# RWKV inverses kept with their halves exchanged, their increments issued in four array quadrants alternately

## The chip, the core and the metric

The kernel runs on one core of a Trainium2 chip. The metric is device time in microseconds (us) of one execution. The kernel before took 2090.66 us, the median of three runs (2089.09 to 2099.26). A change of 0.5% is 10.5 us.

A core has five engines with instruction queues of their own: TensorE (PE; its weight loads are shown as PEld), VectorE (DVE), ScalarE (ACT), GpSimd (POOL) and SyncE (SP, which issues transfers). They wait for each other through semaphores. TensorE writes to PSUM, eight banks of 512 fp32 columns on 128 partitions, and DVE and ACT read PSUM.

## What is computed

The program runs two blocks, one after the other. The first mixes a gated MLP branch and an RWKV-7 branch; the second has a latent attention (MLA) layer and a state-space (S5) layer. The change touches the RWKV-7 branch alone, whose core is a recurrence over 512 tokens for 8 heads of width 64:

```python
def step(S, inp):
    r_t, w_t, k_t, v_t, a_t, b_t = inp
    sa = jnp.einsum('bhij,bhj->bhi', S, a_t)
    S = S * w_t[:, :, None, :] + sa[..., None] * b_t[:, :, None, :] + v_t[..., None] * k_t[:, :, None, :]
    y = jnp.einsum('bhij,bhj->bhi', S, r_t)
    return S, y
```

## The kernel before

**Chunks and units.** The recurrence is cut into 8 chunks of 64 tokens. Inside a chunk it becomes products of 64x64 matrices and the inverse of a unit triangular one. Two heads make a unit (`q` or `i`, 0 to 3), and inside it `e` (0 or 1) is the head. For one head the 8 chunks lie as 4 pairs (`tt`), the even chunk of a pair on partitions 0 to 63, the odd one on 64 to 127, so a tile of 128 x 256 holds eight 64x64 matrices.

**A quadrant.** A 64x64 matmul uses a quarter of the 128x128 array: the 64 rows on which its operands lie, and the 64 columns that lead to the output's partitions. Here "0 to 1" means operands on partitions 0 to 63 and the output on 64 to 127.

**The inverse.** `products_pe` computes, for each chunk, the matrix A in both orientations and two products with r. `z0_dve` and `zt0_dve` mask the near diagonal of A, add the identity, and so start the inverse Z and its transpose ZT, kept in one tile `ZZ` (index 0 and 1). Then five levels double the block size of the inverse. At each level `u_pe` multiplies the masked A (`AL`, made by POOL) by Z, 8 matmuls for each head; ACT copies the result to `UA` (`u_act_`); `dz_pe` makes the increments of Z and ZT from `UA` and `ZZ`, 8 matmuls each for each head; and DVE adds both to `ZZ` in one operation of 512 columns (`dz_dve`, L1344). At level 5 only ZT is needed. At level 2 `u_pe` also multiplies `AKT` by v into the other half of the same bank, and one copy of 512 columns (L1283) takes both. `akt_pe` makes AKT into the place of the products once DVE has read them.

**Two quadrants, four quadrants.** All these level matmuls go through `turns` (L1193): even chunk 0 to 0, odd chunk 1 to 1, and so on alternately, so only two of the four quadrants are used. `product_pe` (L1177) goes over both heads and both chunk parities in turn: its operands lie on half `e` and its output on half `odd`, so it uses all four quadrants, and writes the two heads' results to two banks.

**Banks.** Before, X of head e (A, then the increments) is bank e and Y of head e (the transposed A, then U) is bank 2 + e.

**Order of work.** The order on every engine is written out by hand in `rwkv_pe`, `rwkv_act`, `rwkv_dve` (L1519, L1582, L1630). Between the steps of unit i stand the state recurrence of unit i - 1 (`state_pe`, `state_dve_`, one step for each chunk), the operands of unit i + 1 (`prep_...`), the normalisation of unit i - 2 (`gn_...`) and pieces of a vector times matrix product that the second block needs (`vec_rows_pe`, L337: 32 small matmuls of about 1 us, from weights that SP loads into a ring). Engines run their queues in order, so an instruction that waits holds all behind it.

Of the kernel before, what the change touches and what calls it, by code (L numbers as in the profile page):

```python
# [20 lines left out]
P = 128  # L21
# [162 lines left out]
def build(nc, io, known):  # L184
# [6 lines left out]
    with memory:  # L191
# [971 lines left out]
        def products_pe(pe, q):  # L1163
# [13 lines left out]
        def product_pe(b, a, lhs, rhs):  # L1177
            for c in range(NCHUNK):
                tt, odd = divmod(c, 2)
                cs = slice(c * CHUNK, (c + 1) * CHUNK)  # L1180
                for e in range(2):
                    ins = nc.tensor.matmul(psum[half(odd), b + e, a + tt * CHUNK:a + (tt + 1) * CHUNK], lhs[half(e), cs], rhs[half(e), cs],
# [3 lines left out]
        def akt_pe(pe, q):  # L1186
# [4 lines left out]
            pe_count.up("rw", q, "AKT")  # L1191

        def turns(b, a, lhs, rhs):  # L1193
            for tt in range(TT):
                for odd in range(2):
                    ins = nc.tensor.matmul(psum[half(odd), b, a + tt * CHUNK:a + (tt + 1) * CHUNK], lhs(half(odd), tt), rhs(half(odd), tt),  # L1196
                                           start=True, stop=True)
            return ins

        def u_pe(pe, q, level):  # L1200
            for e in range(2):
# [7 lines left out]
                if level == 2:  # L1209
                    pe.wait_ge(*at("rw", q, ("U_copied", 1), e))  # L1210
                    pe.wait_ge(*at("rw", q, "AKT_masked", e))
                    turns(2 + e, 256, lambda h, tt: AKT[h, tt, :], lambda h, tt: tms[q % 2][h, tt, 3, half(e)])
                pe.wait_ge(*at("rw", q, ("AL", level), e))
                turns(2 + e, 0, lambda h, tt: AL[h, level % 2, tt, :], lambda h, tt: ZZ[h, 0, tt, :]).then_inc(pe_done, 1)
                pe_count.up("rw", q, ("U", level), e)

        def dz_pe(pe, q, level):
            for e in range(2):
# [5 lines left out]
                if level < LEVELS:  # L1224
                    turns(e, 0, lambda h, tt: ZZ[h, 1, tt, :], lambda h, tt: UA[h, 0, tt, :])
                turns(e, 256, lambda h, tt: UA[h, 0, tt, :], lambda h, tt: ZZ[h, 1, tt, :]).then_inc(pe_done, 1)
                pe_count.up("rw", q, ("dZ", level), e)

        def w_pe_(pe, q):
            for e in range(2):  # L1230
# [3 lines left out]
                for tt in range(TT):  # L1234
                    for part in range(2):
                        for odd in range(2):
                            h = half(odd)
                            src = tms[q % 2][h, tt, 0, half(e)] if part == 0 else UA[h, 1, tt, :]
                            ins = nc.tensor.matmul(psum[h, 2 + e, tt * P + part * HEAD:tt * P + (part + 1) * HEAD], ZZ[h, 1, tt, :], src,
# [3133 lines left out]
```

## Time and profile before

| | |
|---|---|
| median of three runs | 2090.66 us |
| the profiled execution's own time | 2087.72 us |
| its span, first to last instruction | 2085.9 us |
| instructions in the span | 42823 |
| the four RWKV units | about 205 to 397 us of the span |
| TensorE busy over the span | 1970.8 us (94%) |
| VectorE busy over the span | 1509.0 us (72%) |

A row of the timeline gives the start in us from the span's start, the time to the end of the last of the merged instructions, the engine, the line of the kernel, the operation, output and inputs, their shapes and the count; in brackets stand the idle time ahead of it and who ended it. An fp32 matmul of the program shows as two passes, each a weight load (PEld) and a MATMUL (PE): 8 matmuls are x16. Their ends are modelled, so a rate is read from the distance between starts.

### The profile page before, as it was taken

The numbers are of one execution on the slowest core, as the hardware profiler recorded it, in microseconds if no ns is written. First come the engines' busy times: TensorE is split into PE (matmuls) and PEld (weight loads), VectorE is DVE, ScalarE is ACT, GpSimd is POOL, SyncE is SP. The second block draws the span as 40 slices with busy tenths as digits, with TensorE's granted clock in tenths as the row PEclk, the third lists the DMA queues.
The fourth block names the chain that finished last, engine by engine and source line by source line (L and its number), as shares of the span: only waits on it lengthen the run. The fifth ranks groups of instructions, "written<-read, shape, count | busy, mean of one in ns | idle before, by whom it ended". The sixth has DMA issues, their size and how long they took to land.

```text
span 2085.9 us, 42823 instructions
## 1 busy us (share of the span) xinstructions
PE 1970.8 (94%) x17574; PEld 1609.5 (77%) x17574; DVE 1509.0 (72%) x2103; ACT 912.9 (44%) x1540; POOL 516.6 (25%) x419
## 2 busy tenths in 40 slices
PE   7999898899999999999999979999989999999997
PEld 6787777777885656655579958888767799999885
DVE  3366665468994677688869866888884789898844
ACT  3325543344324444444465365555443544343423
POOL 2553221140005999300001121111111111111000
PEclk9999999999999999999999989999999999999998
DMA  9222344332452222112138858999964433333321
GB/s 366 86 92 71 124 144 144 145 133 74 157 191 92 71 91 86 61 64 79 66 136 327 294 217 236 311 305 303 323 206 167 142 102 102 103 104 114 137 91 41
DMA packets 127507, 317.89 MB, mean 152 GB/s; under 512 B 12129, under 2 KB 59105, under 8 KB 120913
## 3 DMA queue, kind: packets, MB, share of 16 engines
q1 hardware_dynamic: 114048, 248.65, 35.7%
q0 software_dynamic: 10672, 53.14, 7.0%
q10 hardware_dynamic: 2592, 13.37, 1.6%
q8 instruction: 140, 2.29, 0.4%
q14 instruction: 55, 0.44, 0.1%
HBM read 238.69 MB, written 76.41 MB: 151 GB/s over the span
## 4 chain that ended last, share of the span: by engine, by line
PE 78%; DVE 10%; issue 4%; ACT 4%; DMA 3%; POOL 1%; SPq 1%; ACTq 0%; POOLq 0%; DVEq 0%
PE psum L524 15%; PE psum L3785 14%; PE psum L2017 7%; PE psum L3209 5%; PE psum L2983 5%; PE psum L2640 5%; PE psum L2603 3%; PE psum L1196 3%; PE psum L2615 2%; PE psum L3379 2%; PE psum L337 2%; PE psum L3438 1%; PE psum L3329 1%; PE psum L2691 1%; PE psum L3185 1%
## 5 line engine op out<-in xcount | busy, mean ns | idle before, releaser
L3209 PE MATMUL psum<-h,u_w 128*128 128x256 f32 (+1 forms) x768 | 157.5, 349 | 7.3 <-DVE h L3137 5.2
L524 PE MATMUL psum<-h_split,in_w 128*128 128x512 f32 x600 | 139.1, 391 | 1.5 <-POOL in_w L513 1.5
L3209 PEld LDWEIGHTS psum<-h,u_w 128*128 128x128 f32 x768 | 118.0, 190 | 27.1 <-issue 10.9
L3742 POOL TENSOR_TENSOR ring<-ring 128x1024 f32<-128x1024 f32 x16 | 54.1, 3383 | 319.1 <-DVE xT L3736 319.1
L524 PEld LDWEIGHTS psum<-h_split,in_w 128*128 128x128 f32 x600 | 111.8, 188 | 27.3 <-ACT prev L860 2.1
L513 POOL TENSOR_TENSOR u_w<-ring,u_w 128x512 fp32r<-128x512 f32 x42 | 53.9, 1283 | 276.2 <-ACT u_w L501 240.9
L506 DVE TENSOR_TENSOR w_split<-ring,w_split 128x512 fp32r<-128x512 f32 x54 | 40.4, 748 | 86.3 <-ACT w_split L501 85.9
L2017 PE MATMUL psum<-x_high,ring_split 128*128 128x512 f32 x272 | 101.1, 393 | 0.0
L2640 PE MATMUL psum<-area,ckv_tm 128*128 128x512 f32 (+1 forms) x256 | 100.4, 545 | 0.0
L2738 DVE TENSOR_REDUCE early<-psum 128x1 f32<-128x768 f32 (+1 forms) x96 | 74.8, 780 | 32.2 <-PE psum L2615 29.6
L513 POOL TENSOR_TENSOR in_w<-ring,in_w 128x512 fp32r<-128x512 f32 x50 | 77.4, 1548 | 79.2 <-ACT in_w L501 77.0
L524 PE MATMUL psum<-split,w_split 128*128 128x512 f32 x384 | 89.7, 397 | 4.5 <-DVE w_split L506 4.5
L3785 PE MATMUL psum<-split,w_split 128*128 128x256 f32 x688 | 89.5, 283 | 1.3 <-ACT w_split L3756 1.3
L524 PEld LDWEIGHTS psum<-split,w_split 128*128 128x128 f32 x384 | 73.7, 192 | 20.2 <-DVE w_split L506 4.7
L2772 ACT ACTIVATE area<-psum 128x768 f32<-128x768 f32 x64 | 51.9, 811 | 84.6 <-PE psum L2629 83.6
L2640 PEld LDWEIGHTS psum<-area,ckv_tm 128*128 128x128 f32 x256 | 47.4, 190 | 51.3 <-issue 48.9
L3785 PEld LDWEIGHTS psum<-split,w_split 128*128 128x128 f32 x688 | 85.4, 191 | 1.7 <-ACT w_split L3756 1.7
L3785 PE MATMUL psum<-split,x_high 128*128 128x256 f32 x592 | 77.5, 284 | 2.4 <-DVE x_high L3764 2.4
L501 ACT ACTIVATE w_split<-ring 128x512 fp32r<-128x512 f32 x54 | 34.1, 631 | 103.2 <-PE psum L524 100.6
L2017 PE MATMUL psum<-ctx_high,ring_split 128*128 128x256 f32 x272 | 78.3, 288 | 0.0
L3785 PEld LDWEIGHTS psum<-split,x_high 128*128 128x128 f32 x592 | 72.8, 188 | 4.0 <-DVE x_high L3764 2.9
L2017 PE MATMUL psum<-h_low,ring_split 128*128 128x256 f32 (+1 forms) x272 | 70.1, 340 | 0.0
(530 smaller groups left out, 5247.0 us busy)
## 6 DMA issues: line engine op xcount, KB each, us to landing
ring<-in_s_glu SPq DMA_DIRECT2D x64, 512.0 KB, 3.3
ring<-in_w_mod SPq DMA_DIRECT2D x48, 512.0 KB, 5.4
c_pow<-made_c_pow SPq DMA_DIRECT2D x32, 576.0 KB, 5.1
ring<-in_s_in SPq DMA_DIRECT2D x32, 512.0 KB, 6.7
b_pow<-made_b_pow SPq DMA_DIRECT2D x15, 1024.0 KB, 10.5
ring<-in_w_in SPq DMA_DIRECT2D x25, 512.0 KB, 3.3
table<-made_table SPq DMA_DIRECT2D x32, 384.0 KB, 6.6
made_c_pow<-area POOLq DMA_DIRECT2D x10, 1152.0 KB, 5.7
```

Source lines behind the costliest of these rows:

```text
L513: nc.gpsimd.tensor_tensor(rounded(buffer(u, 1)), source(u), buffer(u, 0), ALU.subtract).then_inc(pool_done, 1)
L524: ins = nc.tensor.matmul(out, rounded(buffer(u, w)[:, ks]), values(x, k), start=(first and k == 0 and n == 0), stop=(last and k == UNIT_K ...
L1196: ins = nc.tensor.matmul(psum[half(odd), b, a + tt * CHUNK:a + (tt + 1) * CHUNK], lhs(half(odd), tt), rhs(half(odd), tt), start=True, stop ...
L2017: ins = nc.tensor.matmul(o, weights, h2_part(x, k, a, n), start=(k == 0 and w == 0 and x == 0), stop=(k == KD - 1 and w == 1))
L2603: mm(o, q_abs_of(h, u, q_part), rounded(ckv_parts[c_part][:, a:a + m]), start=(q_part == 0 and c_part == 0), stop=False)
L2640: ins = mm(o, ckv_tm[:, k, :], pt[:, k, :], start=(k == 0), stop=(k == kt - 1))
L2738: v.tensor_reduce(sm[:, n % 3, 0:1], scores_of(n), AX.X, ALU.max).then_inc(dve_done, 1)
L2772: nc.scalar.activation(dst, psum[:, 6:8, 0:3 * P].rearrange("p b (k c) -> p b k c", k=3), ACT.Copy).then_inc(act_done, 1)
L2983: ins = nc.tensor.matmul(mla_out_part(m, a, a + HALF), weights, rounded(values), start=(k == 0 and w == 0 and x == 0), stop=(k == KE - 1 a ...
L3209: ins = nc.tensor.matmul(o, rounded(u_w[:, u % 4, w, kk * P:(kk + 1) * P]), h3_part(x, k)[:, a:a + size], start=(k == 0 and n == 0), stop= ...
L3742: nc.gpsimd.tensor_tensor(left_plain(i, "S3"), left_plain(i, "A11"), left_plain(i, "S3"), ALU.subtract).then_inc(pool_done, 1)
L3785: ins = nc.tensor.matmul(product_of(i, q), left[:, k * P:(k + 1) * P], rounded(rounded_chunks[:, low_n if x else high_n, k, :]), start=(w ...
```

## The change

The transposed A that feeds `AL`, the A that starts Z, and with them `Z` and `AL`, are kept with the chunks of a pair exchanged: the even chunk on partitions 64 to 127. The U product then goes 0 to 1 and 1 to 0 and comes out in the natural places, the increment of Z goes 0 to 1 and 1 to 0 again, and the increment of ZT 0 to 0 and 1 to 1 as before. In `dz_pe` the two increments are now issued alternately, two matmuls of the one and two of the other, into two banks (X of head e is now bank 2e, Y is 2e + 1). ZT stays natural, so it needs a transposed A in the natural places: a fifth product of 16 matmuls (`at_natural_pe`) is computed into X ahead of AKT, and DVE masks it from PSUM instead of from the copy in `AT`. At level 2 the AKT product goes to the bank of X, so ACT copies it apart from U.

```diff
         def X(e, a=0, n=TT * CHUNK):
-            return bank(e, a, a + n)
+            return bank(2 * e, a, a + n)
         def Y(e, a=0, n=TT * CHUNK):
-            return bank(2 + e, a, a + n)
+            return bank(2 * e + 1, a, a + n)
...
             for b, lhs, rhs in ((0, a_cm, b_cm), (2, b_cm, a_cm)):
-                product_pe(b, 0, lhs, rhs).then_inc(pe_done, 1)
+                product_pe(b, 0, lhs, rhs, crossed=True).then_inc(pe_done, 1)
...
+        def at_natural_pe(pe, q):
             for e in range(2):
                 pe.wait_ge(*at("rw", q, "Z0", e))
                 pe.wait_ge(*at("rw", q, "RBT_masked", e))
+            product_pe(0, 0, b_cm, a_cm).then_inc(pe_done, 1)
+            pe_count.up("rw", q, "AT_natural")
+
+        def akt_pe(pe, q):
+            for e in range(2):
+                pe.wait_ge(*at("rw", q, "ZT_masked", e))
             product_pe(0, 0, k_cm, a_cm).then_inc(pe_done, 1)
...
+        def turn(b, a, tt, lhs, rhs, crossed=False):
+            for odd in range(2):
+                to = half(1 - odd if crossed else odd)
+                ins = nc.tensor.matmul(psum[to, b, a + tt * CHUNK:a + (tt + 1) * CHUNK], lhs(half(odd), tt), rhs(half(odd), tt),
+                                       start=True, stop=True)
+            return ins
...
-                    turns(2 + e, 256, lambda h, tt: AKT[h, tt, :], lambda h, tt: tms[q % 2][h, tt, 3, half(e)])
+                    turns(2 * e, 256, lambda h, tt: AKT[h, tt, :], lambda h, tt: tms[q % 2][h, tt, 3, half(e)])
...
-                turns(2 + e, 0, lambda h, tt: AL[h, level % 2, tt, :], lambda h, tt: ZZ[h, 0, tt, :]).then_inc(pe_done, 1)
+                crossed_turns(2 * e + 1, 0, lambda h, tt: AL[h, level % 2, tt, :], lambda h, tt: ZZ[h, 0, tt, :]).then_inc(pe_done, 1)
...
-                if level < LEVELS:
-                    turns(e, 0, lambda h, tt: ZZ[h, 1, tt, :], lambda h, tt: UA[h, 0, tt, :])
-                turns(e, 256, lambda h, tt: UA[h, 0, tt, :], lambda h, tt: ZZ[h, 1, tt, :]).then_inc(pe_done, 1)
+                for tt in range(TT):
+                    if level < LEVELS:
+                        crossed_turn(2 * e, 0, tt, lambda h, tt: ZZ[h, 1, tt, :], lambda h, tt: UA[h, 0, tt, :])
+                    ins = turn(2 * e + 1, 256, tt, lambda h, tt: UA[h, 0, tt, :], lambda h, tt: ZZ[h, 1, tt, :])
+                ins.then_inc(pe_done, 1)
...
                 if level == 2:
-                    nc.scalar.activation(unit["UA", e][:, :, :, :], bank(2 + e).rearrange("p (a t c) -> p a t c", a=2, t=TT),
-                                         ACT.Copy).then_inc(act_done, 1)
-                else:
-                    nc.scalar.activation(unit["UA", e][:, 0, :, :], tt4(Y(e)), ACT.Copy).then_inc(act_done, 1)
+                    nc.scalar.activation(unit["UA", e][:, 1, :, :], tt4(X(e, 256)), ACT.Copy).then_inc(act_done, 1)
+                    act_count.up()
+                nc.scalar.activation(unit["UA", e][:, 0, :, :], tt4(Y(e)), ACT.Copy).then_inc(act_done, 1)
...
         def zt0_dve(dve, q):
             v = nc.vector
+            dve.wait_ge(*at("rw", q, "AT_natural"))
+            for e in range(2):
+                v.tensor_tensor(unit["ZZ", e][:, 1, :, :], tt4(X(e)), over(mask("diag2_upper"), TT), ALU.mult).then_inc(dve_done, 1)
+                dve_count.up("rw", q, "ZT_masked", e)
...
-                v.tensor_tensor(ZT, unit["AT", e][:, :, :], over(mask("diag2_upper"), TT), ALU.mult).then_inc(dve_done, 1)
-                dve.wait_ge(dve_done, dve_count.up())
+                dve.wait_ge(*at("rw", q, "ZT_masked", e))
...
-                    nc.vector.tensor_tensor(ZZ, bank(e).rearrange("p (a t c) -> p a t c", a=2, t=TT), ZZ, ALU.add).then_inc(dve_done, 1)
+                    both_steps = flat(2 * e * BANK, (2 * e + 3) * BANK).rearrange("p (a x) -> p a x", a=2)[:, :, 0:BANK // 2]
+                    nc.vector.tensor_tensor(ZZ, both_steps.rearrange("p a (t c) -> p a t c", t=TT), ZZ, ALU.add).then_inc(dve_done, 1)
...
-            akt_pe(pe, i)
+            at_natural_pe(pe, i)
             if scan:
                 state_pe(pe, i - 1, 1)
+            akt_pe(pe, i)
```

In PE's queue of unit 0, from the decay and rate products (L994, L996) to the end of level 1's increments, before:

```order
L994 MATMUL psum<-wdad,up 128x512
L996 MATMUL psum<-wdad,up 128x512
L1182 MATMUL psum<-a_cm,k_cm 64x64 x16
L337 MATMUL psum<-ring,vectors 32x128 x16
L1196 MATMUL psum<-ZZ,AL 64x64 x16
L1002 MATMUL psum<-const,tmp 128x2 x4
L1196 MATMUL psum<-UA,ZZ 64x64 x8
L1196 MATMUL psum<-ZZ,UA 64x64 x8
L1196 MATMUL psum<-UA,ZZ 64x64 x8
L1196 MATMUL psum<-ZZ,UA 64x64 x8
```

And the same place now, up to the first half of the first head's increments:

```order
L994 MATMUL psum<-wdad,up 128x512
L996 MATMUL psum<-wdad,up 128x512
L1183 MATMUL psum<-a_cm,b_cm 64x64 x16
L1183 MATMUL psum<-a_cm,k_cm 64x64 x16
L337 MATMUL psum<-ring,vectors 32x128 x16
L1203 MATMUL psum<-ZZ,AL 64x64 x16
L1002 MATMUL psum<-const,tmp 128x2 x4
L1203 MATMUL psum<-UA,ZZ 64x64 x2
L1203 MATMUL psum<-ZZ,UA 64x64 x2
L1203 MATMUL psum<-UA,ZZ 64x64 x2
L1203 MATMUL psum<-ZZ,UA 64x64 x2
```

The natural A product stands ahead of AKT, and the runs of 8 have become runs of 2 of the two increments in turn.

In DVE's queue of unit 0, between the first masks of Z (L1315 to L1319) and the scan of unit 1 (L1095), before:

```order
L1326 TENSOR_TENSOR RKT<-psum,const 128x256 x2
L1330 TENSOR_TENSOR ZZ<-AT,const 128x256
L1332 TENSOR_TENSOR ZZ<-ZZ,const 128x256
L1330 TENSOR_TENSOR ZZ<-AT,const 128x256
L1332 TENSOR_TENSOR ZZ<-ZZ,const 128x256
L1336 TENSOR_TENSOR AKT<-psum,const 128x256 x2
L1095 SCALAR_TENSOR_TENSOR g_cm<-const,be_cm 128x512
```

And now:

```order
L1347 TENSOR_TENSOR ZZ<-psum,const 128x256 x2
L1351 TENSOR_TENSOR RKT<-psum,const 128x256 x2
L1356 TENSOR_TENSOR ZZ<-ZZ,const 128x256 x2
L1360 TENSOR_TENSOR AKT<-psum,const 128x256 x2
L1095 SCALAR_TENSOR_TENSOR g_cm<-const,be_cm 128x512
```

The eight operations are as many as before; the masks of ZT now come first and read PSUM, so the group starts with a wait for the new product.

## Rows read from the trace of the kernel before

**Rows 1.** The page, busy time and instructions of each engine.

```profile
PE 1970.8 (94%) x17574; PEld 1609.5 (77%) x17574; DVE 1509.0 (72%) x2103; ACT 912.9 (44%) x1540; POOL 516.6 (25%) x419
```

**Rows 2.** The page, shares of the chain that ended last.

```profile
PE 78%; DVE 10%; issue 4%; ACT 4%; DMA 3%; POOL 1%; SPq 1%; ACTq 0%; POOLq 0%; DVEq 0%
```

**Rows 3.** Windows: us, busy PE, PEld, DVE, ACT, POOL, clock, DMA; RWKV units.

```profile
205.00:397.00 192.00, 166.50 (x4814) 144.77 (x4816) 107.78 (x207) 81.92 (x148) 36.54 (x41) 0.97 0.39 136
```

**Rows 4.** Timeline of PE in unit 0: products, one whole-array matmul, level 4's increments.

```profile
205.95 0.69 PE L1182 MATMUL psum<-b_cm,a_cm 64*64 64x64 f32 x32 [0.78 <-ACT tm L1087]
206.44 0.67 PE L1182 MATMUL psum<-a_cm,b_cm 64*64 64x64 f32 x32
...
230.28 1.13 PE L1031 MATMUL psum<-tmp,const 128*128 128x512 f32 x2
231.34 0.68 PE L1196 MATMUL psum<-UA,ZZ 64*64 64x64 f32 x16
231.85 0.63 PE L1196 MATMUL psum<-ZZ,UA 64*64 64x64 f32 x16
232.32 0.63 PE L1196 MATMUL psum<-UA,ZZ 64*64 64x64 f32 x16
```

**Rows 5.** Timeline of unit 2, levels 1 to 3, PE, DVE and ACT.

```profile
305.68 0.68 PE L1196 MATMUL psum<-UA,ZZ 64*64 64x64 f32 x16
...
306.95 0.69 DVE L1344 TENSOR_TENSOR ZZ<-psum,ZZ 128x512 f32<-128x512 f32 x1 [0.84 <-PE psum L1196]
...
307.81 1.08 PE L337 MATMUL psum<-ring,vectors 128*32 128x128 f32 x32
...
310.02 0.60 ACT L1283 ACTIVATE UA<-psum 128x512 f32<-128x512 f32 x1 [3.58 <-PE psum L1196]
...
311.86 0.68 PE L1196 MATMUL psum<-UA,ZZ 64*64 64x64 f32 x16
...
314.06 0.69 DVE L1344 TENSOR_TENSOR ZZ<-psum,ZZ 128x512 f32<-128x512 f32 x1 [0.24 <-PE psum L1196]
314.30 1.18 PE L1196 MATMUL psum<-ZZ,AL 64*64 64x64 f32 x32
...
315.03 0.38 ACT L1286 ACTIVATE UA<-psum 128x256 f32<-128x256 f32 x1 [3.12 <-PE psum L1196]
...
315.47 0.68 PE L1196 MATMUL psum<-UA,ZZ 64*64 64x64 f32 x16
```

**Rows 6.** Timeline of unit 2 behind level 3's increments, DVE and PE.

```profile
315.77 1.10 DVE L1125 SCALAR_TENSOR_TENSOR tmp<-rkvg,cols,k_new 128x512 f32<-128x512 f32 x1
...
317.24 1.42 DVE L1344 TENSOR_TENSOR ZZ<-psum,ZZ 128x512 f32<-128x512 f32 x2
...
318.66 1.10 PE L1196 MATMUL psum<-ZZ,AL 64*64 64x64 f32 x32
...
319.69 1.08 PE L337 MATMUL psum<-ring,vectors 128*32 128x128 f32 x32
```

**Rows 7.** Timeline of unit 0's start, from AKT to level 1's increments.

```profile
211.09 0.76 DVE L1326 TENSOR_TENSOR RKT<-psum,const 128x256 f32<-128x256 f32 x2
211.20 0.69 PE L1182 MATMUL psum<-a_cm,k_cm 64*64 64x64 f32 x32 [2.10 <-DVE RBT L1319]
...
212.84 1.15 PE L1196 MATMUL psum<-ZZ,AL 64*64 64x64 f32 x32
...
214.90 0.68 PE L1196 MATMUL psum<-UA,ZZ 64*64 64x64 f32 x16
```

**Rows 8.** Timeline of unit 2's start: the second state step of unit 1.

```profile
304.44 0.33 PE L1376 MATMUL psum<-states,carry 64*64 64x64 f32 x4 [0.92 <-DVE states L1383]
```

**Rows 9.** Waits of PE, 205 to 385 us: total us, times, longest.

```profile
PE psum L1196 <- issue: 5.6, 4, 1.8
```

**Rows 10.** Timeline of unit 1: a stall, and the increments behind it.

```profile
255.49 0.92 PE L1196 MATMUL psum<-ZZ,AL 64*64 64x64 f32 x17 [1.54 <-issue]
...
257.49 1.12 PE L1196 MATMUL psum<-UA,ZZ 64*64 64x64 f32 x16
```

More of the change, by code:

```diff
@@ L1181, in product_pe @@
                 for e in range(2):
-                    ins = nc.tensor.matmul(psum[half(odd), b + e, a + tt * CHUNK:a + (tt + 1) * CHUNK], lhs[half(e), cs], rhs[half(e), cs],
+                    to = half(1 - odd if crossed else odd)
+                    ins = nc.tensor.matmul(psum[to, 2 * e + b // 2, a + tt * CHUNK:a + (tt + 1) * CHUNK], lhs[half(e), cs], rhs[half(e), cs],
                                            start=True, stop=True)
             return ins
-        def akt_pe(pe, q):
+        def at_natural_pe(pe, q):
             for e in range(2):
@@ L1189, in akt_pe, with crossed_turn, crossed_turns @@
                 pe.wait_ge(*at("rw", q, "RBT_masked", e))
+            product_pe(0, 0, b_cm, a_cm).then_inc(pe_done, 1)
[3 more added lines that the diff above has]
+                pe.wait_ge(*at("rw", q, "ZT_masked", e))
             product_pe(0, 0, k_cm, a_cm).then_inc(pe_done, 1)
             pe_count.up("rw", q, "AKT")
+        def turn(b, a, tt, lhs, rhs, crossed=False):
+            for odd in range(2):
+                to = half(1 - odd if crossed else odd)
+                ins = nc.tensor.matmul(psum[to, b, a + tt * CHUNK:a + (tt + 1) * CHUNK], lhs(half(odd), tt), rhs(half(odd), tt),
+                                       start=True, stop=True)
+            return ins
+        def crossed_turn(b, a, tt, lhs, rhs):
+            return turn(b, a, tt, lhs, rhs, crossed=True)
         def turns(b, a, lhs, rhs):
             for tt in range(TT):
-                for odd in range(2):
-                    ins = nc.tensor.matmul(psum[half(odd), b, a + tt * CHUNK:a + (tt + 1) * CHUNK], lhs(half(odd), tt), rhs(half(odd), tt),
-                                           start=True, stop=True)
+                ins = turn(b, a, tt, lhs, rhs)
+            return ins
+        def crossed_turns(b, a, lhs, rhs):
+            for tt in range(TT):
+                ins = crossed_turn(b, a, tt, lhs, rhs)
             return ins
@@ L1223, in dz_pe @@
                 pe.wait_ge(*at("rw", q, ("U_copied", level), e))
[L1224 to L1226 removed]
+                for tt in range(TT):
+                    if level < LEVELS:
+                        crossed_turn(2 * e, 0, tt, lambda h, tt: ZZ[h, 1, tt, :], lambda h, tt: UA[h, 0, tt, :])
+                    ins = turn(2 * e + 1, 256, tt, lambda h, tt: UA[h, 0, tt, :], lambda h, tt: ZZ[h, 1, tt, :])
+                ins.then_inc(pe_done, 1)
                 pe_count.up("rw", q, ("dZ", level), e)
@@ L1238, in w_pe_ @@
                             src = tms[q % 2][h, tt, 0, half(e)] if part == 0 else UA[h, 1, tt, :]
-                            ins = nc.tensor.matmul(psum[h, 2 + e, tt * P + part * HEAD:tt * P + (part + 1) * HEAD], ZZ[h, 1, tt, :], src,
+                            ins = nc.tensor.matmul(psum[h, 2 * e + 1, tt * P + part * HEAD:tt * P + (part + 1) * HEAD], ZZ[h, 1, tt, :], src,
                                                    start=True, stop=True)
```

4 lines of the change are left out of this document (2 added, 2 removed).

## The prediction

> **What bounds the kernel now.** I read the page first. TensorE is busy 94% of the span and nothing else is near it [rows 1], and the chain that ended last runs through PE for 78% and through DVE for 10% [rows 2]. So time that goes out of PE's work is worth something where PE, and not its feeder, is the last to be ready. That has to be read from the stage that changes. The windows view of the four RWKV units shows 192 us, with PE busy 166.5 and DVE 107.8 of them [rows 3]. PE there waits little, but DVE's list is long enough to take over when PE gets faster. What comes behind the stage starts when the stage ends, so I count a gain here in full.
>
> The timeline tells what a quadrant costs. A whole-array fp32 matmul of 512 columns takes two passes, 1.06 us from its start to the next start [rows 4]; scaled to 64 columns a pass would be some 66 ns (estimate). The increments, which use two quadrants, put 16 passes into 0.47 us, 29 ns each. The products, which use four, put 32 passes into 0.49 us, 15 ns each [rows 4]. So the quadrants work beside each other, two in the one case and four in the other.
>
> **The change, part by part.** The sum is made against the profiled execution: 2087.72 us, 2.9 us below the median of 2090.66.
>
> *Increments, levels 1 to 4.* For one unit and level 64 passes at 29 ns become 64 at 15 ns: 1.86 us become 0.93. PE alone would gain 4 units x 4 levels x 0.93 = 14.9 us. Level 5 makes ZT alone and stays on two quadrants. What arrives at the end of a level I walk through unit 2, where the state steps, the next operands and the old normalisation all stand between. From the rows: DVE starts 1.27 us after a head's increments start, so 0.34 after the last pass is issued; its add takes 0.69, with some 0.04 to the next when both heads are ready; the copy comes 0.73 after U starts, lasts 0.38, and the next increments follow 0.06 later [rows 5]. PE follows a DVE result by about 0.13 (AKT at 211.20, after the DVE operation that made way for the one at 211.09 [rows 7]).
> - Level 1. The filler product L337 stands behind the increments and takes 1.0 us [rows 5]. With T the start of the increments, the adds now end at T + 0.47 + 0.34 + 0.69 = T + 1.50 and T + 2.23, and the filler ends at T + 0.93 + 0.2 + 1.0 = T + 2.13. U's second head starts after T + 2.23, so nothing new is late: the whole 0.93 is gained.
> - Level 2. Behind it stands no long filler. U of head 0 starts at T + 1.63, of head 1 at T + 2.36, and PE is through with it at T + 2.83; the state step follows, so level 3 starts at T + 3.0. Before it took 311.86 to 315.47 = 3.61 [rows 5]. Gain 0.6: the rest is lost to the chain PE, DVE, PE, ACT.
> - Level 3. DVE is the late one. From the end of level 2's adds (314.75) it works through two operations for the next unit, two state steps and a small add, until level 3's adds end at 318.66: 3.9 us that don't change [rows 5, 6]. So these adds end 0.93 + 0.62 = 1.55 earlier. U's two heads were issued together behind them, up to L337 at 319.69; now the first goes ahead and the second ends about 0.6 after the adds: L337 starts 1.97 earlier, which makes the gain of this level 0.4.
> - Level 4. DVE's list is as long again, and I take 0.2, between 0 and 0.9.
>
> Together 2.2 us for a unit. Unit 0 has no state steps on DVE, so its levels should give more: 3.0, between 2.2 and 3.7.
>
> *The natural A product.* It stands where AKT stood, and takes 0.47 us at the rate of the products; AKT must now also wait until DVE has masked it. In unit 0 AKT started at 211.20 and DVE went on at 211.09 [rows 7]. Now DVE waits for the new product until 211.20 + 0.47 + 0.34 = 212.0, masks two heads (2 x 0.38, from the 0.76 of a pair in rows 7) until 212.8, and AKT starts at 212.9: 1.7 us later, which reaches level 1 at 214.90 in full, because PE had no gap between. In units 2 and 3 the normalisation of an older unit keeps DVE busy meanwhile, and PE waited 0.92 us further on for the state step [rows 8]: this takes up the 1.0 us by which U1 is later. Cost 0 there; if that cover were gone, 1.0 each. Unit 1 has no normalisation but has the state step: 0.3.
>
> *DVE and ACT.* DVE has the same eight operations at the start, and the add over two banks has as many columns as before: 0 (if reading two banks cost a pair 0.1 us more, 16 pairs would give 1.6). At level 2 one copy of 0.60 becomes two of 0.38 [rows 5], 0.2 us later for each head. In units 0 to 2 a product of 1.0 us stands between U and the increments and hides it. In unit 3 it does not, and costs up to 0.5; but there DVE has little else to do and levels 3 and 4 give about that much more, so I keep 2.2.
>
> *Queues.* No transfer is added or moved. SP's ring loads are released by the ends of L337 and come a little earlier.
>
> *Sum.* Unit 0: -3.0 + 1.7 = -1.3. Unit 1: -2.2 + 0.3 = -1.9. Units 2 and 3: -2.2 each. In all -7.6 us. ZT's mask and add also no longer follow each other directly, which takes about 0.1 us of waiting out of DVE's list in each unit: I take -8, that is -0.4%. On the profiled execution's 2087.72 that is 2079.7, on the median 2090.66 it is 2082.7. The runs that count are medians, so I say 2082.
>
> **Rivals.**
> - *Two heads' worth of rows in one bank do not run together in four quadrants.* In every run of four quadrants in this trace, the operands of one half of the partitions go to one bank and those of the other half to another. In the new run both halves write to one bank at a time, as the two-quadrant runs do. If the pairs with a common bank exclude each other, the run stays at 29 ns a pass, the levels give nothing, and the costs remain: 1.7 + 0.3 + up to 0.5 = 2.5 us slower, 2093. The levels are worth 3.0 + 3 x 2.2 = 9.6 us in my sum, so from the point where the quadrants give less than about a quarter of it, the change loses. Against it: in the two-quadrant runs the halves do share a bank and still work beside each other (29 ns against 66), and for two outputs on the same partitions the new order uses two banks, as the products do. If all passes excluded each other (66 ns), the levels would cost 16 x 64 x 0.037 = 38 us more and the time would be 2131; nothing in the rows speaks for it. The Trainium skill has a rule that speaks for this rival: in "TensorEngine Tiling (Array Packing)", Gotcha 1, matmuls whose operands lie on different row tiles cannot write the same PSUM bank at the same time. By that rule the time is the 2093 above. The 29 ns of the old runs, which break it on different partitions, disagree.
> - *PE runs out of instructions.* PE stood still four times in the level products for "issue", 5.6 us in all and 1.8 at the longest, with nothing in the profile to wait for [rows 9]. Faster runs use up instructions sooner, and 64 matmuls are added. If each unit got one more such stall of 1.4 us (5.6 over 4), 5.6 us of the gain would go: 2088. For it: these stalls lie in dense runs. Against it: the average rate rises by only 4%. The Trainium skill, in "Runtime: NRT & Kernel Launch", Instruction fetch mechanics, calls the cost of a fetch mostly hidden. By that the 2082 would stand; the stalls of rows 9 say it is not always so.
> - *The clock falls.* The stage has a mean clock of 0.97 [rows 3]. In unit 1, after a stall of 1.54 us, the first 16 passes of the increments lasted 1.12 us instead of 0.68 [rows 10, 5]: the 1.2 GHz level instead of 2.4. The start of a unit now has two waits of PE close together. If in two more units 1.86 us of full-clock work ran at half the clock, that would cost 3.7 us: 2086. Against it: a wait of 2.10 us stood at the start of unit 0, and the increments behind it kept the full level (0.68 again) [rows 7].
> - *PE alone decides.* If the chains overlap better than I walked, the gain is 14.9 less the four new products of 0.47 = 13.0: 2077.7. Against it stand DVE's 3.9 us in level 3.
>
> **How the numbers follow.** 2082 and its neighbourhood, 2077 to 2086: 0.60. Instructions or clock take back part of it, 2086 to 2091: 0.19. PE alone, 2075 to 2078: 0.10. Banks exclude, near 2093: 0.09; fully serial, 2131: 0.02. The range 2076 to 2091 leaves out the last two and some of the edges. A measurement of this kernel can tell about 0.5%, 10.5 us, from no change: faster than that means below 2080.2. I give it a third of the main case and nearly all of the "PE alone" case, 0.29 in all; slower than 2101 is the serial case, 0.02; the rest, 0.69, is no change that can be told.
>
> **What would show it.** In the profile after, L1203's runs should put 64 passes of a level's increments into some 0.93 us; at 1.86 the bank rival holds. In unit 0 AKT should start near 212.9 if the units before it stand as now; in units 2 and 3 the second state step should start without PE's wait of 0.92. Behind level 3 PE should now wait for DVE's adds. The waits for "issue" in the level products should stay near 5.6 us. The forecast is wrong if the stage of 192 us gets shorter by less than 4 or more than 12 us.

## The result: slower, and the profile after

The changed kernel took 2101.6 us (median of 20 runs, 2094.0 to 2106.3), the kernel before 2090.4 (20 runs, 2082.8 to 2099.3). The ratio is 1.0046, with a 95% interval of 1.0035 to 1.0057: 0.35 to 0.57% slower, some 11 us by the medians. Forecast were 2082 and a range up to 2091. The profiled execution of the changed kernel took 2099.68 us.

The four units took 193.3 us before, from the first product at 205.95 to the first matmul of L524 at 399.24; now they take 207.1, from 204.50 to 411.57. They start 1.45 us earlier than before, and what stands behind them is as long as it was.

The page of the changed kernel, as [rows 1] and [rows 2], with its instruction queue (packets, MB, share):

```profile
PE 1972.9 (94%) x17702; PEld 1605.4 (77%) x17702; DVE 1507.6 (72%) x2103; ACT 913.7 (44%) x1548; POOL 514.7 (25%) x419
...
q8 instruction: 141, 2.31, 0.4%
...
PE 78%; DVE 10%; issue 4%; ACT 3%; DMA 2%; POOL 1%; SPq 1%; ACTq 0%; DVEq 0%; POOLq 0%
```

Nothing here tells the loss: busy times and the chain are as before. The windows view of the same stretch as [rows 3] does, and so do two stretches inside it:

```profile
205.00:397.00 192.00, 158.57 (x4765) 133.02 (x4758) 103.14 (x196) 78.05 (x148) 32.94 (x40) 0.90 0.35 124
...
211.50:214.90 3.40, 3.40 (x72) 2.80 (x74) 3.25 (x7) 0.00 (x0) 0.00 (x0) 0.51 0.02 5
303.70:313.90 10.20, 9.82 (x187) 8.68 (x181) 5.32 (x12) 3.13 (x5) 1.45 (x2) 0.50 0.02 5
```

PE is busy 8 us less in the same 192 us. Part of this is the denser runs themselves, which need less of its time. But the clock is 0.90 instead of 0.97: PE spends stretches at the lower of its two levels. Read in windows of 1 us, these stretches add up to some 44 us of the stage, 14 in the kernel before.

The waits of PE in the stage (total us, times, longest), as [rows 9]:

```profile
PE psum L1203 <- issue: 8.7, 7, 3.1
PE psum L1183 <- DVE RBT L1340: 6.1, 4, 2.1
PE psum L1044 <- issue: 3.9, 2, 2.9
PE psum L1183 <- DVE ZZ L1347: 3.2, 4, 1.0
...
```

All its waits for "issue" from 204 to 400 us add up to 20.6 us; in the kernel before the same sum is 9.3 (the 5.6 of [rows 9] are those in the level products alone). The wait of L1183 for ZZ of L1347, four times 0.8 us, is new: AKT behind the mask of ZT.

The start of unit 0, the place of [rows 7], in the timeline of PE and, in the fence behind it, of DVE:

```profile
207.07 0.59 PE L996 MATMUL psum<-wdad,up 64*128 64x512 f32 x1
209.77 0.69 PE L1183 MATMUL psum<-a_cm,b_cm 64*64 64x64 f32 x32 [2.12 <-DVE RBT L1340]
211.50 1.14 PE L1183 MATMUL psum<-a_cm,k_cm 64*64 64x64 f32 x32 [1.03 <-DVE ZZ L1347]
212.56 1.93 PE L337 MATMUL psum<-ring,vectors 128*32 128x128 f32 x32
...
216.71 0.27 PE L1203 MATMUL psum<-UA,ZZ 64*64 64x64 f32 x2
216.72 0.27 PE L1203 MATMUL psum<-ZZ,UA 64*64 64x64 f32 x2
...
217.64 0.23 PE L1203 MATMUL psum<-ZZ,UA 64*64 64x64 f32 x2
```

```profile
210.60 0.76 DVE L1347 TENSOR_TENSOR ZZ<-psum,const 128x256 f32<-128x256 f32 x2 [0.97 <-PE psum L1183]
```

The unit itself starts 1.45 us earlier than before, so AKT at 211.50 is 1.7 us later in its unit, just as forecast. But its 32 passes now take 1.06 us to the next start, and L337 takes 1.87 to the next start instead of the 1.0 of [rows 5]: between 207.7 and 211.5 PE was busy 0.7 us at the full clock, and from 211.5 on the granted clock was 0.51. The increments then do run in four quadrants: 64 passes from 216.71 to 217.64, 0.95 us, as in the products.

A stall behind "issue" in unit 1: the timeline of PE, and the transfers of two windows (tenths of busy DMA in 40 slices, then queues with packets and MB), first 278.0 to 281.4, then 280.4 to 281.4:

```profile
278.78 0.86 PE L1203 MATMUL psum<-ZZ,UA 64*64 64x64 f32 x23
282.70 0.45 PE L1203 MATMUL psum<-ZZ,UA 64*64 64x64 f32 x9 [3.06 <-issue]
```

```profile
DMA  7877899989999979989897998282932201010103
...
q1 hardware_dynamic: 261, 0.93, 67.7%
q8 instruction: 1, 0.02, 1.7%
...
DMA  0900470700033000003000003000003000000900
...
q1 hardware_dynamic: 19, 0.05, 15.0%
q8 instruction: 1, 0.02, 5.7%
```

PE stops in the middle of a run of level 5. The engines of the DMA are full of the ring's loads (q1) till about 280.4; only then does one packet of the instruction queue q8 move, and it is through by 281.4. PE goes on 1.3 us later. That the queue is PE's is read from the counts. The page of the kernel before has this line for it:

```profile
q8 instruction: 140, 2.29, 0.4%
```

The kernel before has 17574 matmuls and as many loads, the changed kernel 256 instructions more and one packet more, so a packet holds some 251; the runs below have 141 or 140 packets just as they have these instructions or not. Two other long stalls of the stage, which end at 336.49 and 372.44, look alike: PE goes on 1.3 to 1.6 us after the end of a q8 packet, with 190 to 260 packets of q1 in the 2.5 to 3.4 us about it.

So three things stood against the levels: a later start of the units, a lower clock behind waits, and more time without instructions. The experiments are to give each its price.

### The profile page after: what moved, and what is told of

It reads as the page before. It is cut to its first block, busy times and chain, and to the rows that moved or that the text cites. A ratio compares the mean times of both kernels' runs of the same rounds, so it can differ in the third digit from the quotient of the medians.

```text
span 2097.9 us, 43091 instructions
## 1 busy us (share of the span) xinstructions
PE 1972.9 (94%) x17702; PEld 1605.4 (77%) x17702; DVE 1507.6 (72%) x2103; ACT 913.7 (44%) x1548; POOL 514.7 (25%) x419
## 4 chain that ended last, share of the span: by engine, by line
PE 78%; DVE 10%; issue 4%; ACT 3%; DMA 2%; POOL 1%; SPq 1%; ACTq 0%; DVEq 0%; POOLq 0%
PE psum L524 15%; PE psum L3811 14%; PE psum L2043 7%; PE psum L3235 5%; PE psum L3009 5%; PE psum L2666 5%; PE psum L2629 3%; PE psum L2641 2%; PE psum L1203 2%; PE psum L337 2%; PE psum L3405 2%; PE psum L2717 1%; PE psum L3464 1%; PE psum L3355 1%; PE psum L2655 1%
## 5 line engine op out<-in xcount | busy, mean ns | idle before, releaser
L524 PE MATMUL psum<-h_split,in_w 128*128 128x512 f32 x600 | 139.0, 391 | 1.5 <-POOL in_w L513 1.5
L524 PEld LDWEIGHTS psum<-h_split,in_w 128*128 128x128 f32 x600 | 111.8, 188 | 27.3 <-ACT prev L860 2.1
L524 PE MATMUL psum<-split,w_split 128*128 128x512 f32 x384 | 89.8, 397 | 4.5 <-DVE w_split L506 4.5
L524 PEld LDWEIGHTS psum<-split,w_split 128*128 128x128 f32 x384 | 73.8, 193 | 20.3 <-DVE w_split L506 4.7
## 6 DMA issues: line engine op xcount, KB each, us to landing
b_pow<-made_b_pow SPq DMA_DIRECT2D x15, 1024.0 KB, 10.5
```

The source lines that it names most:

```text
L524: ins = nc.tensor.matmul(out, rounded(buffer(u, w)[:, ks]), values(x, k), start=(first and k == 0 and n == 0), stop=(last and k == UNIT_K ...
```

## The experiments

Each was timed in five rounds against the kernel before on the same chip. The changed kernel was not in these rounds, so a difference from it is given by the ratios and by the medians. "Issue" is the sum of PE's waits for issue from 204 to 400 us, "clock" the granted clock from 205 to 397 us, both of the one profiled run.

**The increments one after the other again** (all else as changed):

```diff
-                for tt in range(TT):
-                    if level < LEVELS:
-                        crossed_turn(2 * e, 0, tt, ...)
-                    ins = turn(2 * e + 1, 256, tt, ...)
+                if level < LEVELS:
+                    crossed_turns(2 * e, 0, ...)
+                ins = turns(2 * e + 1, 256, ...)
```

> The changed kernel with the two increments of a head issued one after the other again (8 matmuls of Z's in the crossed quadrants, then 8 of ZT's in the straight ones); the exchanged halves, the natural A product and the two copies at level 2 stay. Theory A (dense runs use up instructions faster than they are fetched beside the ring loads, PE stalls and its clock falls): the increments are back at 1.86 us for a level, PE's issue waits in the stage go from about 20 us back to about 11, the stage's clock from 0.90 to 0.96 or more, and the time is 2 to 5 us above before, 0.2% at most, so 6 to 9 below the changed kernel. Theory B (the new waits at a unit's start lower the clock): the clock stays near 0.90 and the time is at or above the changed kernel's, 10 us or more above before.

2095.1 us, ratio 1.0032 (1.0014 to 1.0051), issue 16.7, clock 0.92. The edit does not bring back the old runs. The 64 passes of a level take 1.49 us to the next start, between the 2.0 of the kernel before and the 1.1 of the changed one, because the runs of Z and of ZT, in different quadrants, overlap (unit 0, increments of level 1):

```profile
221.61 0.51 PE L1203 MATMUL psum<-UA,ZZ 64*64 64x64 f32 x10
221.90 0.27 PE L1203 MATMUL psum<-ZZ,UA 64*64 64x64 f32 x2
...
223.10 1.08 PE L337 MATMUL psum<-ring,vectors 128*32 128x128 f32 x32
```

With less dense runs the kernel gets faster by 3 us (ratios) to 6 (medians), which theory B excluded; but issue and clock stay far from the 11 us and the 0.96 of theory A. Both expectations missed, and neither theory stands alone. What the old runs would give here, this run does not tell.

**AKT behind the first half of the vector rows:**

```diff
-            akt_pe(pe, i)
             vec_rows_pe(pe, n0, EARLY, ...)
+            akt_pe(pe, i)
```

> The changed kernel with the AKT product moved behind the vector rows (L337), so that PE works while DVE masks ZT. PE's 3.2 us of waits for that mask go. Theory A: the stalls stay, the time falls by 1 to 4 us against the changed kernel and is still 6 us or more above before. Theory B: the stretches of half clock at the units' starts go with the wait, the stage's clock rises to 0.95 or more, and the time falls by 8 us or more, to before or below.

2094.4 us, ratio 1.0026 (1.0012 to 1.0040), issue 19.8, clock 0.91. This is 4 us (ratios) to 7 (medians) below the changed kernel, between the two expectations: the second wait of the start is worth something, and that is not the whole loss.

**Short ring loads, in the changed kernel and in the kernel before.** The weights of the vector products come as 512 KB pieces; here 128 floats of each row are loaded, so most of `w_ada` and `w_mod` is missing from the result:

```diff
-                    sp.dma_start(ring[:, n % RING, 0:floats], io[tensor][i]).then_inc(slot_loaded[n % RING], 16)
+                    short = 128 if tensor in ("w_ada", "w_mod_0", "w_mod_1") else floats
+                    sp.dma_start(ring[:, n % RING, 0:short], io[tensor][i][:, 0:short]).then_inc(slot_loaded[n % RING], 16)
```

> The changed kernel, with each ring load of the modulation weights cut to its first 128 floats a row (64 KB instead of 512 KB); the vector products then use stale weights, everything is issued as before. Theory A, with the ring loads as what delays the fetches: PE's issue waits in the stage fall from about 20 us to under 6, the clock is 0.96 or more, and the time falls by 14 us or more against the changed kernel, to 4 us or more below before. Theory B or a fetch that is slow by itself: issue waits stay above 12 us and the time stays within 5 us of the changed kernel.

> The kernel before with the same cut of the ring loads. Theory A: its issue waits of about 11 us fall to under 4 and the time falls by 5 to 9 us; the changed kernel with the same cut is then about 8 us below this one, which is the gain that was forecast. If the loads have nothing to do with the stalls: no change, within 2 us of before.

2077.4 us changed (0.9948, 0.9932 to 0.9964), 2076.9 before (0.9944, 0.9922 to 0.9965). Issue falls from 20.6 to 3.8 and from 9.3 to 1.5. The loads thus cost the changed kernel 24 us and the kernel before 13. In the profiled runs the four units get shorter by 21.1 and 7.5 us, the waits for issue by 16.8 and 7.8. The clock rose to 0.92 only, not to the 0.96 that theory A expected. And with most of the stalls gone the kernels are equal, the four units too (186.0 and 185.8 us), where theory A expected 8 us between them: the levels' gain still doesn't show. Unit 1 says why. The timeline of PE, the kernel before with short loads (first product, AKT, L337, level 1's increments, W):

```profile
248.20 0.69 PE L1182 MATMUL psum<-b_cm,a_cm 64*64 64x64 f32 x32
...
254.56 1.13 PE L1182 MATMUL psum<-a_cm,k_cm 64*64 64x64 f32 x32 [1.59 <-DVE RBT L1319]
...
255.83 1.93 PE L337 MATMUL psum<-ring,vectors 128*32 128x128 f32 x32
...
259.97 0.68 PE L1196 MATMUL psum<-UA,ZZ 64*64 64x64 f32 x16
...
284.05 0.33 PE L1239 MATMUL psum<-tm,ZZ 64*64 64x64 f32 x4
```

and the changed kernel with short loads:

```profile
247.99 0.69 PE L1183 MATMUL psum<-b_cm,a_cm 64*64 64x64 f32 x32
...
254.37 1.13 PE L1183 MATMUL psum<-a_cm,b_cm 64*64 64x64 f32 x32 [1.96 <-DVE RBT L1340]
256.53 1.13 PE L1183 MATMUL psum<-a_cm,k_cm 64*64 64x64 f32 x32 [0.81 <-DVE ZZ L1347]
257.59 1.93 PE L337 MATMUL psum<-ring,vectors 128*32 128x128 f32 x32
...
262.16 0.27 PE L1203 MATMUL psum<-UA,ZZ 64*64 64x64 f32 x2
...
284.01 0.33 PE L1261 MATMUL psum<-tm,ZZ 64*64 64x64 f32 x4
```

From level 1's increments to W it is 24.1 us before and 21.9 now: the forecast 2.2. From the first product to the increments it is 11.8 before and 14.2 now. Read in the same way, the four units gain 2.9, 2.2, 1.9 and 2.8 in the levels (9.8 in all) and lose 2.9, 2.4, 2.8 and 2.4 at the start (10.5). Of the 10.5, 1.7 are fetches still: the products wait 3.0 us for issue, 1.3 in the kernel before. With all loads the stretch from level 1's increments to W is shorter by only 0.7 us in the four units together: there most of the levels' gain goes to the stalls.

**AKT issued twice in the kernel before** (64 instructions more on PE for a unit, no new wait):

```diff
+            product_pe(0, 0, k_cm, a_cm)
             product_pe(0, 0, k_cm, a_cm).then_inc(pe_done, 1)
```

> The kernel before with the AKT product issued twice in each unit: 64 more PE instructions in a unit, at the place where the change adds as many, and no new wait (0.47 us of PE work each). Theory C (the added instructions move and multiply the points at which PE runs out of fetched instructions beside the ring loads): issue waits in the stage go from 9 us to 15 or more, and the time is 5 us or more above before. Theory D (the costs come from the new wait at the unit's start alone): issue waits stay within 3 us of before's and the time is 1 to 3 us above before.

2099.0 us, ratio 1.0028 (1.0013 to 1.0044), issue 13.7. Four products of 0.5 us are 2 us of work; by the ratio the time rose by 6, by the medians of that chip by 8, as theory C expected. The waits for issue rose by 4.4, less than it expected and more than theory D did. Added instructions cost more than their own time here.

**No natural product.** ZT starts from the exchanged copy, as the old line did, so the inverse isn't the wanted one; PE and DVE start a unit as before, and the increments run in four quadrants:

```diff
-            at_natural_pe(pe, i)
+            akt_pe(pe, i)
...
+                v.tensor_tensor(ZT, unit["AT", e][:, :, :], over(mask("diag2_upper"), TT), ALU.mult)
```

> The changed kernel without the natural A product and its wait: ZT starts from the copied, exchanged A as in the kernel before (so the inverse is not the inverse). The PE instructions and the start are those of before, the increments run in four quadrants. Theory C and theory D both have the start's cost gone (10 us or more); they differ in the stalls: C, issue waits back at 8 to 12 us and the time 6 to 10 us below before; if instead the dense runs make the stalls (theory A), issue waits stay at 15 us or more and the time is within 4 us of before.

2092.1 us, ratio 1.0008 (0.9994 to 1.0022), issue 17.4. With the start's cost gone and the levels fast, the time is that of the kernel before: 8.1 us more of waits for issue stand against the 9.8 of the levels. This is what was expected if the dense runs make the stalls, and theory C, with 6 to 10 us of gain, missed. Here the dense runs do give the gain back to the fetches. Issue, each time of one profiled run, is thus 9.3 in the kernel before, 13.7 with 64 matmuls more, 17.4 with dense runs and 20.6 with both.

**Ring loads paced.** SP waits for a step of the unit ahead of three loads of a burst, in the changed kernel and in the kernel before (left out here is the table `paced`, which says which load waits for which step):

```diff
+                    if n in paced:
+                        sp.wait_ge(*at(*paced[n]))
                     sp.dma_start(ring[:, n % RING, 0:floats], io[tensor][i]).then_inc(slot_loaded[n % RING], 16)
```

> The changed kernel with the same ring loads, each but the first of a burst held back by SP until a named step of the unit is done, so that they come singly and not four in a row. If fetches wait behind bursts of loads, issue waits fall from 20 us to under 10 and the time falls by 6 us or more against the changed kernel; if any load beside a fetch delays it as much, issue waits stay above 15 us and the time within 3 us.

> The kernel before with the same pacing. If bursts are what delays the fetches: issue waits fall from 9 us to under 5 and the time is 3 to 9 us below before; else within 2 us of it.

2085.4 us changed (0.9971, 0.9958 to 0.9985), issue 8.9; 2086.2 before (0.9980, 0.9966 to 0.9994), issue 5.5. Spread over the unit, the same bytes cost the changed kernel 16 us less and the kernel before 5 (its issue was expected under 5). So it is the bursts, more than the volume, that make PE wait for its instructions; the waits are still longer than with short loads (3.8 and 1.5). In what way a load delays a packet, no run shows. From the first product to level 1's increments and from there to W, the paced pair says what the short one said: 9.1 us lost, 10.9 gained.

**An earlier start.** DVE takes the masks of Z and RBT of both heads first and adds the identity behind them, masks ZT right after, and AKT stands behind the vector rows. Once with all loads, once with short ones (as above), once paced, and for a control the kernel before with the same order of masks, paced:

```diff
             for e in range(2):          # written short
-                (mask Z; add the identity; mask RBT)
+                (mask Z; mask RBT)
+            for e in range(2):
+                (add the identity)
+            dve.wait_ge(*at("rw", q, "AT_natural"))
+            for e in range(2):
+                (mask ZT)
```

> The changed kernel with the start of a unit rewritten: DVE masks Z and RBT of both heads first and adds the identity afterwards, so the natural product waits for four DVE operations instead of six; ZT is masked right behind it; and the vec_rows product stands between the natural product and AKT. Ring loads as they are. Theory S+F (the loss is the start of the units, some 2.6 us each, plus instruction fetches behind the bursts of ring loads): the start gets 1 to 2.5 us a unit shorter, the issue waits of the stage stay at 15 us or more, and the time is 2090 to 2096, not below the kernel before by more than 3. Theory S alone (the start is all that was lost): 2080 to 2085 with issue waits near 9. Theory N (neither; the new runs themselves cost the time): within 2 us of the 2094.4 of the kernel with AKT late, with the start no shorter in effect.

> The same with the ring loads cut to 128 floats a row (most of w_ada and w_mod is left out of the result). There the two kernels took 2076.9 (before) and 2077.4 (changed). Theory S (the levels do give about 2.2 us a unit, and the start took it back): first product to level 1's increments goes from 12.7 to 14.8 us down to 11 to 13, W of a unit comes 1.5 to 2.5 us earlier than in the changed kernel with short loads, and the time falls to 2068 to 2073. Rival L (the levels' gain is given back by the chain whatever the start does): 2075 to 2078.

> The same start, with the ring loads of a burst paced by steps of the units. Theory S+F: both losses are tended, so 2077 to 2082, that is 4 to 8 us below the paced changed kernel (2085.4), issue waits 6 to 11 us; faster than both kernels. Rival: the start's gain runs into the fetches that are left (issue waits 12 or more) and the time is 2084 to 2088.

> A control: the kernel before with the same order of masks on DVE (Z and RBT of both heads first, the adds behind) and the same pacing; AKT stays where it was. Theory S+F: AKT starts about 1.2 us earlier and some of it reaches the end of each unit: 2082 to 2086 (2086.2 with pacing alone), so the increments in four quadrants are worth 3 to 6 us between this run and the changed kernel with both. Rival: the order of the masks is what is worth the time, and this run is as fast as that one, within 1.5 us; then the change gives nothing even where its start and its fetches are tended.

With all loads 2094.0 (1.0022, 1.0009 to 1.0035), issue 21.9; short 2076.8 (0.9935, 0.9919 to 0.9951); paced 2081.1 (0.9965, 0.9951 to 0.9980); the kernel before, paced, 2086.4 (0.9986, 0.9972 to 1.0000). The first is what theory S+F expected, but theory N as well, and no faster than AKT late alone (2094.4). The paced pair came out nearly as expected (the kernel before 0.4 us outside its range, the changed one with issue 11.8 instead of at most 11): 5 us between them, and the order of masks by itself is worth nothing to the kernel before. The short one missed what the theory of the start expected, 2068 to 2073. From the first product to W its units 0 and 1 were 3.5 and 3.0 us faster than those of the changed kernel with short loads; in units 2 and 3 the state step waited 1.84 and 2.48 us, until the old normalisation was through, and AKT stood behind it.

**AKT ahead of the state step in units 2 and 3**, once short and once paced:

```diff
             at_natural_pe(pe, i)
+            if i > 1:
+                akt_pe(pe, i)
             if scan:
                 state_pe(pe, i - 1, 1)
             vec_rows_pe(pe, n0, EARLY, ...)
-            akt_pe(pe, i)
+            if i <= 1:
+                akt_pe(pe, i)
```

> The early start with short ring loads (most of w_ada and w_mod left out of the result), but in units 2 and 3 AKT goes ahead of the state step and of vec_rows, as DVE masks ZT before it turns to the old normalisation; units 0 and 1 stay as in the early start. There level 1's increments began 13.8 and 13.0 us behind the first product in units 2 and 3, against 11.0 and 10.3 in the kernel before, and W came 0.9 and 2.3 us later. Theory S (the start alone takes the levels' gain back in units 2 and 3 too): the increments begin 10.5 to 12.5 us in, W of units 2 and 3 comes 0.5 to 2 us earlier than in the kernel before with short loads (35.1 and 31.7), and the time is 2070 to 2075, against 2076.8 to 2077.4 of the three others. Rival L (a unit in full service gives the gain back in its chain or clock): W of units 2 and 3 stays at 35 and 32 or later, and the time is 2075 to 2078.

> The same order with all loads, paced. Theory S+F: 1 to 5 us below the early start with pacing (2081.1), so 2076 to 2080, the fastest complete kernel. Rival L: 2080 to 2084.

Short 2074.1 us (0.9910, 0.9886 to 0.9934), within the 2070 to 2075 expected, if near their end. The start of unit 2 there, in the timeline of PE:

```profile
286.96 0.69 PE L1183 MATMUL psum<-b_cm,a_cm 64*64 64x64 f32 x32
...
292.83 0.69 PE L1183 MATMUL psum<-a_cm,b_cm 64*64 64x64 f32 x32
294.57 0.69 PE L1183 MATMUL psum<-a_cm,k_cm 64*64 64x64 f32 x32 [1.05 <-DVE misc L359]
295.37 0.44 PE L1402 MATMUL psum<-inject,carry 64*64 64x64 f32 x4
295.74 1.08 PE L337 MATMUL psum<-ring,vectors 128*32 128x128 f32 x32
...
299.04 0.27 PE L1202 MATMUL psum<-ZZ,UA 64*64 64x64 f32 x2
```

AKT and L337 run at the full clock again, the increments begin 12.1 us in, and W follows 34.3 us in, 0.8 earlier than in the kernel before with short loads. Unit 3 remained 1.1 us slower than there, behind a wait for issue of 1.40 in its products; its expectation missed. Paced, with all loads, this kernel took 2080.4 us (0.9950, 0.9934 to 0.9966; 12 runs, 2077.6 to 2086.9), at the border of its two expectations. It is the fastest complete one by its median, not to be told from the early start with pacing (2081.1): 10 us faster than the kernel before, some 6 faster than the kernel before with the pacing alone.

## Why the prediction was wrong

**The step that failed** is the one on the natural product: 1.7 us in unit 0, "0.3" in unit 1, "Cost 0 there" in units 2 and 3, 2.0 in all. With short loads the start lost 2.9, 2.4, 2.8 and 2.4 us, 10.5 in all, or 8.8 without the waits for issue in the products. By itself this leaves about 1 of the 8 us that were forecast. It has two parts.
- *The cover was counted, the queue was not.* I let the old normalisation keep DVE busy "meanwhile" and let PE's later wait of 0.92 [rows 8] take up what was left. But ZT's masks stand behind that normalisation in DVE's queue, AKT waits for them, and L337 and U stand behind AKT on PE. Unit 2 with short loads, in the timeline of PE, the kernel before and then the changed one:

```profile
292.82 0.69 PE L1182 MATMUL psum<-b_cm,a_cm 64*64 64x64 f32 x32
...
300.52 1.15 PE L1196 MATMUL psum<-ZZ,AL 64*64 64x64 f32 x32
302.58 0.33 PE L1376 MATMUL psum<-states,carry 64*64 64x64 f32 x4 [0.91 <-DVE states L1383]
```

```profile
293.26 0.69 PE L1183 MATMUL psum<-b_cm,a_cm 64*64 64x64 f32 x32
...
295.98 0.28 PE L1183 MATMUL psum<-rkvg,b_cm 64*64 64x64 f32 x4 [1.16 <-issue]
...
301.90 1.13 PE L1183 MATMUL psum<-a_cm,k_cm 64*64 64x64 f32 x32 [0.46 <-DVE ZZ L1347]
302.96 1.93 PE L337 MATMUL psum<-ring,vectors 128*32 128x128 f32 x32
304.83 0.58 PE L1203 MATMUL psum<-ZZ,AL 64*64 64x64 f32 x5
```

U starts 11.6 us in instead of 7.7: 1.2 of that is a wait for issue in the products, 1.4 is the clock (below), and the rest is the new product and AKT's wait. The 0.92 was indeed used up, as the prediction asked, and 2.8 came through.
- *The clock.* In unit 0 with all loads AKT was late by the 1.7 forecast, and AKT and L337 at half the clock (1.06 and 1.87 us instead of 0.6 and 1.0) took 1.3 more. L337 behind a unit's start ran at the lower level in 11 of 12 starts of the changed kernel (all loads, short, paced) and in 2 of 12 of the kernel before (in one more for a part). The prediction let one row of the kernel before with one wait, [rows 7], stand against this rival. Two waits with one product between them are new, but they are not the rule: the kernel before with short loads fell behind one wait in units 0 and 1 (2.11 us, and the 1.59 shown above), and the changed kernel with all loads kept the full clock behind two in its unit 1:

```profile
251.91 0.69 PE L1183 MATMUL psum<-a_cm,b_cm 64*64 64x64 f32 x32 [1.39 <-DVE RBT L1340]
...
253.63 0.72 PE L1183 MATMUL psum<-a_cm,k_cm 64*64 64x64 f32 x32 [0.91 <-DVE ZZ L1347]
254.28 1.08 PE L337 MATMUL psum<-ring,vectors 128*32 128x128 f32 x32
```

Why one start falls and another does not stays open.

**The levels** came out in sum, 9.8 us measured with short loads and 9.6 in the prediction, but the parts did not, so the size is in part luck. In unit 2 levels 1 to 4 gave 1.14, 0.57, -0.35 and 0.52 us instead of 0.9, 0.6, 0.4 and 0.2. At level 2, AKT times v in the straight quadrants now overlaps with U in the crossed ones, 64 passes in some 1.6 us instead of 2.0, which the sum lacked. Behind level 3 PE waited at L337 for a small add of DVE that stands ahead of the level's own adds in DVE's queue:

```profile
317.62 1.08 PE L337 MATMUL psum<-ring,vectors 128*32 128x128 f32 x32 [1.01 <-DVE misc L361]
```

The mechanism holds: the runs reach 15 ns a pass although both halves write one bank, so the rival of the banks falls. The Trainium skill's "TensorEngine Tiling (Array Packing)", Gotcha 1, says that different row tiles cannot access one bank at the same time; 64 passes in 0.95 us here disagree with it, for outputs on different partitions.

**PE runs out of instructions** was named, with one more stall of 1.4 us a unit, 5.6 in all. The waits grew by 11.3 (9.3 to 20.6). "Against it: the average rate rises by only 4%" was the weak link: the runs with short and with paced loads show that it matters when the next packet lands, and what the ring loads do then. I read [rows 9] without asking what the transfers did in those stalls. The Trainium skill, in "Runtime: NRT & Kernel Launch", Instruction fetch mechanics, calls the cost of a fetch mostly hidden; that nearly holds with short loads (1.5 us in the stage before, 3.8 in the changed one) and not beside 512 KB bursts.

**The sum.** -9.8 for the levels, +8.8 for the start, +11.3 for issue gives +10; the four units grew by 13.8 in the profiled runs, and the medians differ by 11. The terms come from different runs and overlap (a stall ahead of a wait for DVE costs less), so this is a check and no proof. The rivals of instructions and clock were each priced alone and given 0.19 together; they came together, since a stall also leaves PE idle: behind the one that ends at 282.70 the clock is at the lower level from 283 to 287. What stays open is how much of the clock's loss belongs to the stalls and how much to the start's waits with all loads; no run held the clock and let the stalls be. The time at the lower level also differs from run to run: 33 and 23 us with short loads, and 34 in the kernel before with pacing and early masks, which is no slower than with pacing alone.

Of the other signs: PE was to wait for DVE's adds behind level 3, and such waits (L1203 for ZZ of L1369) don't show in the changed kernel and come to 0.7 us with short loads, beside the wait of L337 above; the waits for issue in the level products didn't stay near 5.6 but came to 8.7; and the stage should have got shorter by 4 to 12 us and got longer by 13.8.

## What to carry to other kernels

A new product on a busy engine costs its own time plus every instruction that stands behind its consumer: follow the wait through both queues, the feeder's and the engine's, before calling it covered. Where PE shows waits for "issue", look at the transfers of that moment: here a denser stream of small matmuls beside bursts of loads paid for its speed in late instruction packets, and spacing the loads (5 us for the kernel before, 16 for the changed one) was worth more than the denser runs. New waits at a place where the engine has little to do are to be priced with the clock at half for what follows as one case, even where the trace before shows a wait there without it.

## What the runs showed of the hardware

- Ring loads of 512 KB in bursts delayed PE's instruction packets: 9.3 and 20.6 us of waits for issue in 196 us, 1.5 and 3.8 with loads of 64 KB in their place, 5.5 and 8.9 with the same loads spaced. In three long stalls PE went on 1.3 to 1.6 us after the packet's end.
- Four 64x64 quadrants ran 15 ns a pass with two outputs sharing a bank on different partitions, as fast as with separate banks. Two runs of 8 matmuls, one in the straight and one in the crossed quadrants, overlapped also when issued one after the other: 64 passes in 1.49 us instead of 2.0.
- At unit 0's start in the changed kernel the granted clock fell to 0.51 after 3.8 us in which PE was busy 0.7, and stayed there 3.4 us though PE was busy throughout (3.40 of 3.40). In the kernel before it stayed at 1.00 there behind a single wait of 2.10 us, and with short loads it was 0.50 behind a single wait of 2.11.
